# A hybrid decoder layer: the front computed transposed, and w_in loaded in six transfers instead of eleven

## What is computed

```
mod = silu(c) @ w_ada + b_ada                 # 6 x 1024: sh1 sc1 gt1 sh2 sc2 gt2
h = rmsnorm(x, g_mix) * (1 + sc1) + sh1
z = h @ w_in                                  # 2816 columns: q k v | q_h f_h i_h g_h
o_a = rmsnorm(window attention with sinks, 8 query heads, 2 key heads of 64)
o_h = rmsnorm(HGRN2 gated linear recurrence, 4 heads 128 x 128) * silu(g_h)
x = x + gt1 * (concat(o_a, o_h) @ w_out)
h = rmsnorm(x, g_ffn) * (1 + sc2) + sh2
x = x + gt2 * moe(h)                          # top 4 of 32 experts, clamped SwiGLU
y = rmsnorm(x, g_final)
```

## Time and profile before

| | us |
|---|---|
| median of three executions | 1313.72 |
| the profiled execution, its own time | 1313.6 |
| its span in the profile | 1311.9 |
| first product of the expert loop starts | 352.75 |
| first chunk issued from inside the loop | 358.24 |
| last products on a newly landed chunk start | 1290.15 |
| PE busy | 1169.4 |
| DVE busy | 368.5 |
| ACT busy | 172.4 |

### The profile page before, as it was taken

How to read it: one execution, slowest core, us unless ns; L and a number is a source line. 1 busy time by engine, 2 the same in 40 slices (tenths; PEclk the granted TensorE clock), 3 DMA queues, 4 the chain that set the end, 5 groups by cost and what they waited for, 6 DMA issues and landing times.

```text
span 1311.9 us, 15212 instructions
## 1 busy us (share of the span) xinstructions
PE 1169.4 (89%) x5976; PEld 483.8 (37%) x5976; DVE 368.5 (28%) x773; ACT 172.4 (13%) x316; POOL 73.1 (6%) x112
## 2 busy tenths in 40 slices
PE   3699778796499999999899999989899999989896
PEld 0388665455233333323232323323232323233232
DVE  1310337546413222122222122121222221221224
ACT  2100443101101101010110101010100101010102
POOL 5000120111000000000000000000000000000000
PEclk8599969897599999999999999999999999999998
DMA  9833338614599999999999999999999999999991
GB/s 355 301 129 129 104 95 343 237 39 148 229 382 430 430 431 430 431 429 431 430 430 431 430 432 430 431 429 431 431 430 432 429 432 428 432 430 431 431 420 58
DMA packets 52304, 464.38 MB, mean 354 GB/s; under 512 B 7467, under 2 KB 18811, under 8 KB 24308
## 3 DMA queue, kind: packets, MB, share of 16 engines
q1 hardware_dynamic: 43936, 444.12, 81.1%
q0 software_dynamic: 6976, 15.76, 3.7%
q10 hardware_dynamic: 1366, 4.15, 0.8%
HBM read 463.57 MB, written 5.85 MB: 358 GB/s over the span
## 4 chain that ended last, share of the span: by engine, by line
PE 64%; DMA 27%; DVE 4%; ACT 2%; issue 1%; ACTq 0%; SPq 0%; DVEq 0%; POOLq 0%
PE bank L1137 32%; DMA ring<-in_w_up 22%; PE bank L779 6%; PE bank L1041 6%; PE bank L1130 4%; PE bank L1158 3%; PE bank L730 3%; DMA ring<-in_w_ada 2%; PE bank L930 2%; DMA arena<-in_w_down 2%; PE bank L868 1%; PE bank L1047 1%; PE bank L747 1%; PE bank L787 1%; PE bank L831 1%
## 5 line engine op out<-in xcount | busy, mean ns | idle before, releaser
L1137 PE MATMUL bank<-ring,arena 128*64 128x512 f32 x1536 | 362.7, 604 | 16.5 <-DMA ring<-in_w_up 14.1
L1137 PEld LDWEIGHTS bank<-ring,arena 128*64 128x64 f32 x1536 | 98.0, 137 | 258.1 <-issue 213.9
L730 PE MATMUL bank<-const,arena 128*128 128x128 f32 (+4 forms) x426 | 72.2, 315 | 67.2 <-DVE arena L1507 14.0
L1158 PE MATMUL bank<-arena 128*64 128x512 f32 x512 | 116.1, 597 | 17.8 <-DMA arena<-in_w_down 17.8
L1158 PE MATMUL bank<-ring,arena 128*64 128x512 f32 x512 | 116.3, 596 | 0.0
L1137 PE MATMUL bank<-arena 128*64 128x512 f32 x512 | 116.1, 595 | 0.0
L1667 DVE TENSOR_SCALAR arena<-bank 128x256 f32<-128x256 f32 x64 | 24.2, 420 | 290.6 <-PE bank L1137 290.6
L730 PEld LDWEIGHTS bank<-const,arena 128*128 128x128 f32 (+4 forms) x426 | 58.7, 201 | 102.3 <-issue 48.5
L1041 PE MATMUL bank<-arena,mods 128*128 128x512 f32 (+2 forms) x204 | 94.4, 629 | 0.0
L694 ACT ACTIVATE arena<-arena 128x512 f32<-128x512 f32 x32 | 20.2, 630 | 500.7 <-DVE arena L1667 500.7
L1657 DVE TENSOR_TENSOR x<-x,bank 128x512 f32<-128x512 f32 x64 | 44.0, 688 | 148.4 <-PE bank L1041 148.4
(11 more groups left out here) (294 smaller groups left out, 773.9 us busy)
## 6 DMA issues: line engine op xcount, KB each, us to landing
ring<-in_w_up SPq DMA_DIRECT2D x96, 2048.0 KB, 24.4
arena<-in_w_up SPq DMA_DIRECT2D x32, 2048.0 KB, 25.1
ring<-in_w_down SPq DMA_DIRECT2D x32, 2048.0 KB, 22.6
arena<-in_w_down SPq DMA_DIRECT2D x32, 2048.0 KB, 24.0
ring<-in_w_ada SPq DMA_DIRECT2D x24, 1024.0 KB, 7.8
ring<-in_w_in SPq DMA_DIRECT2D x11, 1024.0 KB, 10.2
ring<-in_w_out SPq DMA_DIRECT2D x4, 1024.0 KB, 6.2
arena<-in_state_hgrn POOLq DMA_DIRECT2D x8, 256.0 KB, 5.5
```

Of the source, the lines that this page charges most:

```text
L730: return pe.transpose(out, in_, ident[0:rows, 0:rows])
L1137: mm = pe.matmul(B[2 * e + c % 2][64 * a:64 * a + 64, :], lhsT=xT[:, k, 64 * e:64 * e + 64], rhs=big(n)[:, CH * r + 512 * c:CH * r + 512 * ...
L1158: mm = pe.matmul(B[4 + e][64 * a:64 * a + 64, :], lhsT=gT[e].rearrange("p (j a t) -> p j a t", j=4, a=2)[:, k % 4, k // 4, :], rhs=big(n). ...
```

## The change

The layout of the front is turned: tokens lie along the free dimension, and features on the partitions.

- x is transposed first, before any norm (24 transposes, with a copy by VectorE and a square by ScalarE each 128 features); the sum of squares over features is a product with a matrix of ones (`ss1`), and its root and reciprocal are taken for 264 tokens on all partitions. Scale and shift are turned into columns (`modT1`), so that modulating is one operation with a scalar per partition for each 128 features. The row spreading, the small transfer of the sample rows and the transposes after modulating go.
- w_in is loaded in the order f, q_h, k and v, q, i, g: six transfers, five of 512 columns (2 KB runs, 2 MB) and one of 256 (`ZORDER`, `ZFIRST`).
- q_h, k, v, q and g (14 blocks of 128 columns) are computed by `by_column` and `attention_queries` with the weights stationary and all 264 tokens moving. f and i stay with the tokens stationary (`by_token`), 256 columns moving; their samples by `decode_rows`.
- The recurrence's levels treat both tiles at once and only the half of the columns that the level's mask keeps, and stand between the blocks of z, as do the rotary products (`rotate`, a product with a permutation) and, between the blocks of g, the scores. The probabilities are divided by their sums before they are turned. The 16 further w_ada chunks come after z.
- The norms of both groups are sums by products with ones, then root and reciprocal over 4 x 264 and 264 elements per partition; w_out is stationary, for all 264 tokens (64 products in two groups of four banks). The second norm's factor is applied after the router product and when the rows h2 are made: 24 products with the unit matrix, and products of one row for the shift. Samples and prompt go through all of this together.
- The rows of the first pair of experts are made by 24 products from h2 on the chip instead of the indirect transfer. x is transposed back into its row layout (24 transposes).
- GpSimd issues the states' stores ahead of the router's weights, after `ow3`, the last update of the states, which VectorE makes after `att_ready`. TensorE waits for the router's weights (`router_full`) ahead of w_out, for a small product `cw` of them with the shift.
- PSUM banks are handed over by name: `take` waits until the last reader has emptied the bank, `give` says it is filled. 

The core of the diff (`take`, `give`, `filled`, `emptied` as said; `bank` gives the named bank; `release` counts up `chunks_used`):

```diff
+ZORDER = (5, 6, 3, 4, 2, 0, 1, 7, 8, 9, 10)
+ZFIRST = (0, 2, 4, 5, 7, 9)
...
-            for c in range(NZ):
-                room(Z0 + c)
-                if c == 3:
-                    sp.wait_ge(sem("mod_rows0_full"), 64)
-                sp.dma_start(chunk(Z0 + c).rearrange("p (k n) -> p k n", k=KT),
-                             w_in[:, :, c * ZC:(c + 1) * ZC]).then_inc(full[place(Z0 + c)], 16)
+            for n in ZFIRST:
+                c, wide_ = ZORDER[n], z_wide(Z0 + n)
+                room(Z0 + n + wide_ - 1)
+                sp.dma_start(z_chunk(Z0 + n), w_in[:, :, c * ZC:(c + wide_) * ZC]).then_inc(full[place(Z0 + n)], 16)
...
+            pool.dma_start(O["kws"][0, :, WIN - 1].rearrange("b g d -> b (g d)"), kd[0:NB, :]).then_inc(sem("rows_stored"), 16)
+            pool.wait_ge(sem("state_final"), HH)
+            pool.dma_start(O["hgp"][0, 0].rearrange("h k v -> k h v"), st.rearrange("p (h v) -> p h v", h=HH)).then_inc(sem("st_stored"), 16)
+            wait_emptied(pool, "ow3")
...
-            pool.dma_start(scale2, wide(mod_dram[1, 0:1, 0:D], 0, P)).then_inc(sem("mod_rows_full"), 16)
+                pool.dma_start(O["hgs"][0, b].rearrange("h k v -> k h v"), states[:, b]).then_inc(sem("states_stored"), 16)
+            pool.wait_ge(sem("rows_stored"), 16 * 6)
+            pool.wait_ge(sem("att_ready"), 1)
             pool.dma_start(wr, A["w_router"][0].rearrange("(k p) e -> p k e", p=P)).then_inc(sem("router_full"), 16)
...
+            def by_token(names, n, half, after=0):
+                landed(z_first(n))
+                w = z_chunk(n)[:, :, ZC * (n - z_first(n)):ZC * (n - z_first(n) + 1)]
+                for t in range(2):
+                    out = take(names[t]) if half == 0 else bank(names[t])
+                    for k in range(KT):
+                        if n == Z0 and t == 0:
+                            pe.wait_ge(sem("h_ready_a" if k >= 4 else "h_ready_d"), 1 + k % 4)
+                        mm = pe.matmul(out[:, ZC * half:ZC * (half + 1)], lhsT=hT[:, k, P * t:P * (t + 1)], rhs=w[:, k, :],
+                                       start=(k == 0), stop=(k == KT - 1), skip_group_check=True)
+                        if t == 0 and k == 0:
...
+            def by_column(name, n, c0, after=0):
+                landed(z_first(n))
+                pe.wait_ge(sem("h_ready_s"), 1)
+                out = take(name)
+                for k in range(KT):
+                    mm = pe.matmul(out[:, 0:NTOK], lhsT=w_tile(n, c0)[:, k, :], rhs=hT[:, k, 0:NTOK], start=(k == 0), stop=(k == KT - 1))
+                    if k == 0:
+                        release(mm, after)
+                give(mm, name)
...
+                pe.wait_ge(sem("lev_ready"), n)
+                out = take(f"L{n}")
+                for t in range(2):
+                    for hd in range(HH):
+                        own = src[:, hd, P * t:P * (t + 1)]
+                        mm = pe.matmul(out[:, 256 * t + 64 * hd:256 * t + 64 * (hd + 1)].rearrange("p (n m) -> p n m", m=m), lhsT=own,
+                                       rhs=own.rearrange("p (n two m) -> p n two m", two=2, m=m)[:, :, 1, :], start=True, stop=True)
+                give(mm, f"L{n}")
+            def rotate(name, raw_name, j):
+                wait_emptied(pe, raw_name)
...
+            attention_queries(0, after=1)
+            level(1)
+            rotate("rk", "k", 4)
+            attention_queries(1)
+            level(2)
...
+            by_column("g0", Z0 + 9, 0, after=2)
+            out = take("kd")
...
+            scores("sc1_2", 1, 0, 2, 2)
+            scores("sc1_3", 1, 1, 2, 2)
+            by_column("g2", Z0 + 10, 0)
...
+            state(0)
+            recurrence(0)
...
+                mm = pe.matmul(out[:, 0:NTOK], lhsT=ones, rhs=squares_a[:, j, :], start=(j == 0), stop=(j == GRP - 1))
+            give(mm, "as")
+            pe.wait_ge(sem("router_full"), 16)
+            wait_emptied(pe, "modT2")
+            out = take("cw")
             for k in range(KT):
+                mm = pe.matmul(out[0:E, 0:1 + NB], lhsT=wr[:, k, :], rhs=sh2T[:, k, :], start=(k == 0), stop=(k == KT - 1))
+            give(mm, "cw")
+            def project(group, k, outs):
+                landed(WO0 + k // 2)
+                for n, d in enumerate(group):
+                    mm = pe.matmul(outs[n][:, 0:NTOK], lhsT=two(chunk(WO0 + k // 2))[:, k % 2, P * d:P * (d + 1)], rhs=cat[:, k, :],
+                                   start=(k == 0), stop=(k == KT - 1))
+                    if k == KT - 1:
+                        give(mm, f"wo{d}")
+            for group in (range(4), range(4, 8)):
+                outs = [take(f"wo{d}") for d in group]
+                for k in range(KT):
+                    if group[0] == 0 and k == 0:
+                        pe.wait_ge(sem("att_ready"), 1)
+                    if group[0] == 0 and k == 4:
+                        pe.wait_ge(sem("hg_ready"), 1)
+                    project(group, k, outs)
...
+                c, r = divmod(k, UP_ROWS)
+                for t in range(3):
+                    mm = pe.matmul(B[k // 4][:, P * (k % 4):P * (k % 4 + 1)],
+                                   lhsT=h2[0:NT[t], t, :].rearrange("p (c n r) -> p c r n", c=UPS, r=UP_ROWS)[:, c, r, :],
+                                   rhs=G[0:NT[t], t, :, :].rearrange("p e s -> p (e s)"), start=(t == 0), stop=(t == 2),
+                                   skip_group_check=True)
+                if k % 4 == 3:
+                    mm.then_inc(sem("xT_made"), 1)
...
+            link(dve.reciprocal(r_hg, r_hg))
+            hgc = cat[:, 4:8, :].rearrange("p h t -> p (h t)")
+            link(dve.tensor_tensor(hgc, hgc, r_hg, ALU.mult))
+            dve.tensor_tensor(hgc, hgc, gs.rearrange("p h t -> p (h t)"), ALU.mult).then_inc(sem("hg_ready"), 1)
+            wait_emptied(dve, "as")
...
+            link(dve.scalar_tensor_tensor(out=by_half(s2T), in0=by_half(ctmp), scalar=1.0, in1=param(g_ffn_c), op0=ALU.add, op1=ALU.mult))
+            update_states(1, ("ow0", "ow1", "ow2", "ow3"))
+            wait_filled(dve, "cw")
+            dve.tensor_scalar(cw[0:E, :], bank("cw")[0:E, 0:1 + NB], brout[0:E, :], None, ALU.add).then_inc(emptied("cw"), 1)
```

More of the change, by code:

```diff
@@ L304, in big_landed @@
         def big_landed(engine, c, it):
-            n = c % BIGS
-            before = sum(place(m) == n for m in range(PRE))
-            engine.wait_ge(full[n], it * (16 * PER // BIGS) + 16 * (before + c // BIGS + 1))
+            engine.wait_ge(big_full[c % BIGS], it * (16 * PER // BIGS) + 16 * (c // BIGS + 1))
         def big(c):
@@ L628, in _ @@
+            for i in range(2):
+                copy_probs(i)
             act.wait_ge(sem("smax_ready"), 1)
```

1973 lines of the change are left out of this document (1075 added, 898 removed), and 15 rows, old and new, of the table bank_of.

## The result

The changed kernel takes 1280.39 us, the kernel before 1313.66 beside it: ratio 0.974, 95% interval 0.973 to 0.976. That is 33 us less, inside the range, and 9.4 us above the forecast of 1271. Its profiled execution took 1280.38 us with a span of 1278.7.

The account below looks back on a forecast made before the run. The prediction took chains between engines to bound the front, and transfers the loop. Its terms put the loop's first issue at 315.5 us, so 1313.6 - 358.24 + 315.5 = 1270.9 us; range 1249 to 1295.

Parts of the forecast that it names:

- The change leaves bytes and instructions of the loop alone. So the end moves one for one with the first issue in the loop: Expert loop: transfers set its pace, 931.9 us for 186 chunks, so only what comes before its first issue was costed.
- a changed pace there: Warning sign in the loop: a pace other than 60 us pairs and 932 us would make the whole sum wrong.
- Part 1: From the start to the first product of z: at 41.5 us, 16 us earlier than before; other end 48.
- The order on ScalarE that I read as the chain: Before z: lower-bound operations 2.1 and exponential 1.1 precede the copy of w_ada's result, 0.6, in a chain of 8.5 us.
- Part 2: z, recurrence levels and scores: 121 us, to 162.5, including 2.8 us of waiting at the last level.
- the rival of a lasting low clock: Front from level 1 on through w_ada runs at low clock: +91 us, 1362; chance 0.05 with other mishaps past 1318.
- The rule of the Trainium skill that stood beside it: For TensorE in the front: cycling through banks with small pauses can make the clock swing between its levels.
- w_in: Its six transfers ahead of z: counted 0 us, bounds -4 to +4, since nobody waits; the skill's page allowed up to 6.7 less.
- Part 3: State, probabilities, w_ada and samples: from 162.5 to att_ready at 222 us.
- Part 4: New wait for the router's weights ahead of w_out: 17.5 us idle after att_ready, bounds 10 and 25, then cw 1.2.
- Part 5: w_out: 64 products 29.3 us plus 2.4 for the fallen clock, from 240.7 to 272.5.
- Part 6: From w_out to the loop: 39 us, loop at 311.5; first issue 4.0 us later, at 315.5.

Follow-up runs that it names:

- best3: Changed kernel with 256-byte-aligned chunk places, router weights in the cosines' columns, reordered VectorE norms, 128-row shift products, and modulation ahead of the lower bounds: 1251.85 us.
- router_const: Changed kernel with the router weights loaded early into the constants' cosine columns, ahead of the stores and att_ready: 1268.49 us, ratio to before 0.9650.
- full_rows: Changed kernel with the four groups of one-row shift products made as products over all 128 rows: 1277.86 us, ratio to before 0.9748.
- best4: best3 with twelve products of constants, results unread, filling TensorE's wait ahead of w_out: 1246.65 us, ratio to before 0.9520.

## Why the prediction was right, and where not

The direction and the mechanism held; the forecast missed 9.4 us of 1280, of which 7.6 stand in the loop and 1.9 ahead of it. The 1.9 are luck in part: terms that are off by up to 5.4 us cancel. That 40.8 us were gained ahead of the loop is read from the timelines; of the parts of the change only w_in's transfers and the place of the router's weights were tried by themselves. What the turned layout, the halved levels and the pair's rows made on the chip each give is not shown.

- **"The change leaves bytes and instructions of the loop alone. So the end moves one for one with the first issue in the loop"** is the step that failed. Bytes and instructions are the same, addresses are not. The loop took 939.5 us for 931.9, and shifting addresses alone in both kernels showed that these cost the 7.6. The prediction named it as what would make the sum wrong ("a changed pace there"), and gave it no bound.
- **Part 1** (41.5): 40.91. x was transposed from 12.46, w_ada complete at 32.68, reciprocal and product 1.80 and 2.36 us. The order on ScalarE that I read as the chain was it: best3 undid it and z started 3.1 us earlier.
- **Part 2** (121 us): 118.05, with the wait of the last level 2.67 us (2.8). The samples of f and i, put at 3.6, would be 4.1 by the rows named there (8.14 less 7.11, four times); the sum hardly changes. The clock held 0.97 over all of it; the rival of a lasting low clock was wrong here. The rule of the Trainium skill that stood beside it (TensorE: Matmul & The Clock Gate, A second HAM failure mode: psum-queue depth-cycling) did not show in this part, with 765 records cycling through the banks.
- **w_in** (0): shown to be 0 in either kernel. What the Trainium skill's figures (DMA: Bandwidth & Descriptors, Bandwidth) would have given, up to 6.7 us, did not come, since nobody waits; the page gives them for transfers issued from GpSimd, and these are issued by SyncE. Only in best3, with z 3.1 us earlier, did w_in cost 1.2 us.
- **Part 3** (59.5): 57.4, from 158.96 to 216.4. The reciprocal of 1056 took 6.75 us (6.9). The clock fell here for some 7 us (windows of 4 us: 0.54 and 0.61 from 192 to 200), with 32 records of w_ada's products in 5.61 us; of the ten traces with the new front four show this fall, and six keep 1.00 there and take 3.64 us for the same records.
- **Part 4** (18.7 from att_ready to w_out): 21.0. Stores as forecast, 221.36 and 5.96 us. The weights landed 9.2 us after the issue, not the 6.3 of the earlier trace rows: two expert chunks of 2 MB had been issued at 216.43 and the eight stores of 256 KB just ahead, and the queues were busy 0.98 of the time between issue and landing. That is the bandwidth that I had named and not priced; with little queued the same transfer took 2.9 us (router_const).
- **Part 5** (31.8): 30.04. I had 2.4 us for a cold start; it cost some 0.7.
- **Part 6** (39): 44.4, the term that was most mis-sized. The one-row products took 8.4 us for 5.7: that is the clock, which I took as full, since at 1.00 they took 5.8 (full_rows). The pair rows took 9.1 for 6.5, and there the clock makes only 0.4: at 1.00 they took 8.74, 0.36 us a product where I had 0.27. Why they cost more than the 24 unit products (5.97 us for as many records) was not looked into. For the loop's first products too I wrote 4.0 us, "TensorE comes to it working now"; they took 5.26, behind a wait of 1.75, and the first issue came 5.55 us after the start.

Up to the first issue these errors cancel: 317.44 for 315.5. With the measured pace of the loop, the prediction's sum would have been 1278.5.

## What to carry to other kernels

Where a kernel streams with its queues always busy, look at the start addresses of the buffers that take the stream before and after any edit to what is placed ahead of them: 32 bytes cost 0.7% here, and putting all six places on multiples of 256 gained 0.8% on the changed kernel without any other edit. A term that is said to be untouched deserves a bound as much as a changed one, as soon as it is 70% of the time. And a gain ahead of a stretch with short waits and small products must be followed through it: the granted clock took back 6 to 7 us of 18, 50 us behind the edit.

## What was unexpected of the hardware

- The rate of the same 2 MB transfers, all queues busy, was 427 GB/s into places 32 to 128 bytes past a multiple of 256, and 431 on it.
- Products over one row let the granted clock fall to its lower level (1.2 GHz) with TensorE busy in 4.00 of 4 us, in six traces of six; the same instructions over 128 rows held 2.4 GHz, in three of three.
- How long the low level then lasts differs for the same instructions: some 7 us in best4, 17 in the changed kernel and 37 in router_const. The 48 records of the pair rows took 8.74 us at 1.00 and 14.90 when all of them ran at 0.50.
- A transfer of 128 KB landed 2.9 us after its issue with little queued, and 9.2 us after it with two transfers of 2 MB and eight of 256 KB issued in the 11 us before.
